# Hybrid gates projected in four column groups of the array and added by a product; diagonal blocks of the lower matrices gathered by ScalarE in place of GpSimd

## The chip, the cores and the metric

The kernel runs on one core of a Trainium2 chip, as one launch. The metric is the device time of the whole launch in microseconds (us), the median of three runs. One further execution was taken by the hardware profiler; all rows of a trace below come from it.

## The reference, cut to what matters here

The program is a six-layer network over 256 tokens of width 1024, in float32. The change lies in its first layer, the hybrid mixer, which works on 256 latent and 256 context tokens together (512 columns, `T2`). There the input is projected by `w_in`; of the projection, 16 columns are the gates of the delta rule, and the keys, values and gates lead to a triangular solve by chunks:

```python
p = a @ w_in                                     # for the latent and the context tokens
ba = p[..., OFF_BA_A:OFF_Q_B].reshape(bsz, n_tok, 2, 2, A_HEADS)
beta = sigmoid(ba[:, :, 0])                      # 8 columns
g = -exp(a_log) * softplus(ba[:, :, 1] + dt_bias)  # 8 columns
...
lower = where(strict, einsum(kb, kc) * decay, 0.0)
sol = triangular_solve(lower + eye, rhs, lower=True, unit_diagonal=True)
```

Everything behind the first layer (feed-forward layers, a conformer convolution, two HGRN mixers, an mLSTM and an S5 mixer) is unchanged.

## The kernel before, in words

Each engine has one instruction queue that it works off in order; semaphores tie the queues together. Weights stream from memory by SyncE (line 4760) in slabs of 1 MB into a ring of six; slab n is issued when the PE has gone past slab n - 6. Products write into seven PSUM banks that are handed out in turn.

In the first layer the input `a` lies as 8 chunks of 128 features by 512 tokens. `HybridProjection` makes 22 column chunks of 128 outputs, numbered n = 0 to 21: 0 to 3 keys, 4 to 7 queries of the attention, 8 and 9 its keys and values, 10 to 13 queries of the delta rule, 14 to 17 its values, 18 to 21 the readout gate. Each is 8 products in float32 (two instructions each in the trace) of 512 or 256 columns. The order of the work is written out by hand in `tensor`, `scalar`, `vector` and `gpsimd`, and other work is hung in after given n:

- after n = 4 on the PE: `gates` (line 1862), 8 products of 72 output columns by 512 tokens, line 1869. Rows 0 to 7 of the result are the decays, rows 64 to 71 the betas. They stand in one table of 128 weight columns in which both 8-column weights lie 64 apart. Then two sums of squares of heads (line 1850);
- on ScalarE, n = 4 ends with the chunk's copy, a SiLU (`silu`, line 1928), a table load (line 1906), a square (line 1936) and the roots of heads 0 and 1 (lines 1944, 1947). n = 5 is the copy of chunk 5 (line 1898), two squares, and `gate_exps` (lines 1955 to 1963), eight activations on the gates. VectorE finishes them in `gate_values` (lines 2009 to 2011). The PE's next step after chunk 6 and its sums is `columns.turn` (line 2235), which waits for that;
- after n = 8, 9, 11 and 13: `lower.products`, the Gram matrices of the keys. VectorE makes the lower matrices of them in `lower.vector`; those of the backward direction are turned by the PE (line 2327) and copied by ScalarE (line 2375). The last turn stands after n = 14;
- `convolve` (lines 2026 and 2028) is a convolution of five taps over each of 12 chunks on VectorE. Convolution 8 reads chunk 14, convolution 9 chunk 15. ScalarE writes their input with the copy of line 1894;
- after n = 11, 13, 15, 17 and within the attention, the PE works off weight slabs of a modulation: products of 32 output columns in four column groups (`part_rows`, line 268 with `silu_cond`);
- `BlockInverse` inverts the diagonal 32x32 blocks of the 32 lower matrices. GpSimd (POOL) clears areas (lines 2451, 2452), waits for the last lower matrix and its turn, gathers the blocks from `l` into `near` by 4 copies of 32 partitions by 1024 elements (line 2476 via `copy`), clears `a` (line 2459), later `b` (line 2463), and scatters the results back (line 2476 again). VectorE transposes what was gathered in `gather` (line 2489), behind convolution 9, and then runs 31 steps (lines 2515, 2516), partly between the rounds of the attention;
- at the end of the projection ScalarE copies chunk 21, does two SiLUs and loads a table (line 1922). The attention begins there with a copy of turned values (line 2154) and the exponentials of the scores (line 2160), each behind VectorE's maximum of them (lines 2208, 2209). VectorE scales the probabilities (lines 2186, 2190), and the PE turns them.

Of the kernel before, what the change touches and what calls it, by code (L numbers as in the profile page):

```python
# [66 lines left out]

VECTORS = [
# [3 lines left out]
    ("hyb_a_log", 1), ("hyb_dt_bias", 1), ("hyb_g_w", KC * 8), ("hyb_beta_w", KC * 8),  # L72
# [12 lines left out]
    ("time", T), ("future", 2 * P),  # L85
# [337 lines left out]
def over_chunks(ap, n):  # L423

    return ap.unsqueeze(1).broadcast_to([ap.shape[0], n, ap.shape[1]])

# [1301 lines left out]
class HybridProjection(Stage):  # L1728
# [7 lines left out]
    def setup(self):  # L1736
# [22 lines left out]
        self.gate_taken, self.gate_exp = k.counter("gate_taken").events(2)  # L1759
# [17 lines left out]
        for n in range(len(self.chunks)):  # L1777
            self.jobs.append(k.job(self.taken[n]))
            if n == 4:
                self.gate_job = k.job(self.gate_taken)  # L1780
            for i in self.sums_after.get(n, ()):
                self.sum_jobs.append(k.job(self.log_ready[i]))
# [9 lines left out]
    def tensor(self, pe):  # L1792
        k = self.k
        front = k.front
        for n, (job, (_, tokens, _)) in enumerate(zip(self.jobs, self.chunks)):
# [23 lines left out]
            if n == 4:  # L1819
                pe.wait_ge(*front.late_vectors)  # L1820
                self.gates(pe)
                pe.wait_ge(k.consts_loaded, 16)
            for i in self.sums_after.get(n, ()):
                self.sum_head(pe, i)
# [37 lines left out]
    def gates(self, pe):  # L1862
# [3 lines left out]
        rows = KC * 8 + 8  # L1866
        w = self.k.v("hyb_g_w", 0, 2 * KC * 8)
        for c in range(KC):
            mm = pe.matmul(job.ap[0:rows, 0:T2], w[:, 8 * c:8 * c + rows], self.a[:, c, :],
                           start=(c == 0), stop=(c == KC - 1))  # L1870
        mm.then_inc(job.full[0], 1)

    def scalar(self, act):
# [4 lines left out]
        for n, (job, (x, tokens, kind)) in enumerate(zip(self.jobs, self.chunks)):  # L1878
# [28 lines left out]
            for i in self.sums_after.get(n + 1, ()):  # L1907
                self.square(act, i)
            if n == 5:
# [10 lines left out]
            if n == 14:  # L1920
                self.lower.take_turned(act, 3)
        act.preload_act_table_set(EXP_LN)
# [26 lines left out]
    def gate_exps(self, act):  # L1949
# [3 lines left out]
        act.wait_ge(*job.full)  # L1953
# [473 lines left out]
class BlockInverse(Stage):  # L2427
# [8 lines left out]
    def setup(self):  # L2436
# [9 lines left out]
        self.gathered, *self.ready = k.counter("blocks_zero").events(3)  # L2446
        self.turned = k.counter("blocks_turned").events(2)

    def gpsimd(self, pool):
        k = self.k  # L2450
        k.pool.link(pool.memset(self.xc, 0.0))
        k.pool.link(pool.memset(k.spare(W_XC, BLOCK * BLOCK)[:, 0:BLOCK * BLOCK:BLOCK + 1], 1.0))
# [20 lines left out]

    def copy(self, pool, q, done, out, x):
# [11 lines left out]
    def gather(self, dve):  # L2486

        dve.wait_ge(*self.gathered)
# [2397 lines left out]
def pack_vectors(i):  # L4886
# [9 lines left out]

    def states(a):
# [8 lines left out]
    v["hyb_beta_w"], v["hyb_g_w"] = small(i["hyb_w_in"][0][:, 2048:2056]), small(i["hyb_w_in"][0][:, 2056:2064])  # L4906
# [93 lines left out]
```

## Time and profile before

| | us |
|---|---|
| median of three runs | 2289.66 (2287.6 to 2290.04) |
| the profiled execution | 2289.95 |
| its span | 2288.1 |
| PE busy | 2221.1 (97%) |
| VectorE busy | 1617.5 (71%) |
| ScalarE busy | 1156.7 (51%) |
| GpSimd busy | 150.9 (7%) |

A row of the timeline gives the start of a group of like instructions in us from the span's start, the time from its first start to its last end, the engine (PE is the matmul side, PEld its weight loads, DVE VectorE, ACT ScalarE, POOL GpSimd, SPq SyncE's queue), the line, the operation, what it writes and reads, its shape and the count. A bracket tells how long the engine sat idle before it and what ended that. Float32 products stand as two instructions each.

### The profile page before, as it was taken

The page shows a single profiled execution, that of the slowest core. Times are in us where ns is not written, and L with a number is a line of the kernel's source. Part 1 is how long each engine was busy: PE and PEld are TensorE (multiplying, and loading weights), DVE is VectorE, ACT ScalarE, POOL GpSimd, SP SyncE. Part 2 cuts the span into 40 slices and gives each one's busy share as a digit, 9 for nine tenths or more (in the row PEclk, how much of TensorE's full clock was granted, in tenths as well). Part 3 has the DMA queues.
Part 4 walks back from the last instruction along what each step waited for, and adds up shares of the span by engine and source line. Part 5 has one row for each costly group of instructions (what it writes and reads, how often), then busy time and mean ns, then how long its engine had stood idle before and what let it go on. Part 6 is the DMA issues. An engine that isn't in the chain of part 4 may idle for free.

```text
span 2288.1 us, 41418 instructions
## 1 busy us (share of the span) xinstructions
PE 2221.1 (97%) x17332; PEld 2045.9 (89%) x17332; DVE 1617.5 (71%) x2749; ACT 1156.7 (51%) x1937; POOL 150.9 (7%) x142
## 2 busy tenths in 40 slices
PE   7999999999999999999999999999999999999998
PEld 3665979998879999999999989997779999999998
DVE  4398667655977655798557787577988557799654
ACT  3425355443365446756345664345556345957343
POOL 0013000000000000000000000015630000000000
PEclk9999999999999999999999999999999999999999
DMA  8248054555244554414554425552024554514552
GB/s 365 74 198 318 25 215 167 186 185 201 93 166 166 185 185 167 182 56 178 182 182 161 147 93 203 184 221 74 19 94 184 184 184 169 183 54 166 185 184 74
DMA packets 50873, 368.46 MB, mean 161 GB/s; under 512 B 5632, under 2 KB 5888, under 8 KB 6528
## 3 DMA queue, kind: packets, MB, share of 16 engines
q1 hardware_dynamic: 50544, 363.72, 43.1%
q8 instruction: 137, 2.24, 0.4%
q10 hardware_dynamic: 144, 2.10, 0.2%
q14 instruction: 48, 0.39, 0.1%
HBM read 364.75 MB, written 1.05 MB: 160 GB/s over the span
## 4 chain that ended last, share of the span: by engine, by line
PE 81%; DVE 11%; ACT 5%; issue 2%; DMA 0%; SPq 0%; DVEq 0%; POOL 0%; ACTq 0%
PE psum L268 67%; DVE weight_rest L262 2%; PE psum L4515 1%; PE psum L3076 1%; PE psum L4516 1%; ACT weight_parts L226 1%; PE psum L4537 1%; PE psum L3710 1%; PE psum L2726 1%; DVE work L2028 1%; PE psum L4551 1%; DVE work L3540 1%; DVE spare L2516 0%; DVE work L2515 0%; DMA weight_ring<-stream_dram 0%
## 5 line engine op out<-in xcount | busy, mean ns | idle before, releaser
L268 PE MATMUL psum<-input_parts,weight_parts 128*128 128x256 f32 x5184 | 931.6, 283 | 6.4 <-DVE work L1495 1.8
L268 PEld LDWEIGHTS psum<-input_parts,weight_parts 128*128 128x128 f32 x5184 | 799.3, 189 | 11.6 <-issue 5.7
L268 PE MATMUL psum<-input_parts,weight_rest 128*128 128x256 f32 x2592 | 732.6, 283 | 0.0
L262 DVE TENSOR_TENSOR weight_rest<-weight_ring,weight_parts 128x1024 fp32r<-128x1024 f32 x528 | 619.9, 1220 | 149.3 <-ACT weight_parts L226 148.9
L226 ACT ACTIVATE weight_parts<-weight_ring 128x1024 fp32r<-128x1024 f32 x540 | 538.0, 1051 | 122.5 <-PE psum L268 121.7
L268 PEld LDWEIGHTS psum<-input_parts,weight_rest 128*128 128x128 f32 x2592 | 487.8, 188 | 0.0
L268 PE MATMUL psum<-hidden_parts,weight_parts 128*128 128x256 f32 x2496 | 450.8, 283 | 2.6 <-DVE weight_rest L262 1.3
L268 PEld LDWEIGHTS psum<-hidden_parts,weight_parts 128*128 128x128 f32 x2496 | 385.0, 189 | 5.9 <-issue 3.4
L268 PE MATMUL psum<-hidden_parts,weight_rest 128*128 128x256 f32 x1248 | 352.1, 282 | 0.0
L268 PEld LDWEIGHTS psum<-hidden_parts,weight_rest 128*128 128x128 f32 x1248 | 234.9, 188 | 0.0
L1479 ACT ACTIVATE work<-psum 128x256 f32<-128x256 f32 x118 | 45.3, 384 | 352.4 <-PE psum L268 350.0
L1499 DVE TENSOR_TENSOR work<-work,psum 128x256 f32<-128x256 f32 x118 | 49.6, 420 | 212.4 <-ACT work L1479 212.2
L268 PE MATMUL psum<-work,weight_ring 128*128 128x256 f32 (+1 forms) x576 | 155.7, 428 | 0.2 <-ACT work L674 0.2
L268 PEld LDWEIGHTS psum<-work,weight_ring 128*128 128x128 f32 x576 | 108.5, 190 | 42.7 <-issue 31.4
L268 PE MATMUL psum<-raw_parts,weight_parts 128*128 128x258 f32 x576 | 109.5, 291 | 2.4 <-DVE raw_parts L697 2.1
L268 PEld LDWEIGHTS psum<-raw_parts,weight_parts 128*128 128x128 f32 x576 | 92.2, 194 | 4.3 <-issue 3.6
L268 PE MATMUL psum<-raw_parts,weight_rest 128*128 128x258 f32 x288 | 82.8, 287 | 0.0
L262 POOL TENSOR_TENSOR weight_rest<-weight_ring,weight_parts 128x1024 fp32r<-128x1024 f32 x12 | 29.0, 2442 | 669.0 <-ACT weight_parts L226 669.0
L268 PE MATMUL psum<-weight_parts,input_parts 128*128 128x256 f32 x384 | 69.2, 283 | 0.0
L268 PE MATMUL psum<-weight_ring,silu_cond 128*32 128x256 f32 x768 | 51.4, 390 | 14.5 <-DMA weight_ring<-stream_dram 12.0
L3141 DVE SCALAR_TENSOR_TENSOR work<-work,vectors 128x256 f32<-128x256 f32 x161 | 64.4, 478 | 0.0
L3774 POOL MEMSET work<- 128x4096 f32 x2 | 7.1, 3530 | 858.5 <-DVE input_parts L945 661.6
(532 smaller groups left out, 2855.9 us busy)
## 6 DMA issues: line engine op xcount, KB each, us to landing
weight_ring<-stream_dram SPq DMA_DIRECT2D x340, 1024.0 KB, 4.8
constants<-constants_dram SPq DMA_DIRECT2D x1, 2304.0 KB, 17.1
work<-s_bc_dram ACTq DMA_DIRECT2D x1, 2048.0 KB, 9.7
work<-ctx_dram SPq DMA_DIRECT2D x1, 1024.0 KB, 5.3
residual<-x_dram SPq DMA_DIRECT2D x1, 1024.0 KB, 7.3
work<-first_dram SPq DMA_DIRECT2D x1, 1024.0 KB, 14.9
out_dram<-residual SPq DMA_DIRECT2D x4, 256.0 KB, 2.1
vectors<-vectors_dram SPq DMA_DIRECT2D x1, 486.5 KB, 14.3
```

The source lines that it names most:

```text
L226: act.activation(self.parts[:, s % SPLITS, cols], self.ring[:, i % RING, cols], ACT.Identity)\
L262: ins = dve.tensor_tensor(self.rest[:, i % RING, cols], self.ring[:, i % RING, cols], self.parts[:, s % SPLITS, cols].bitcast(F32), ALU.su ...
L268: mm = pe.matmul(*args, **kw)
L1479: act.activation(self.hid[:, j % 2, :], job.early.ap[:, 0:T], ACT.Silu).then_inc(self.silu[j][0], 1)
L1499: dve.tensor_tensor(hid, hid, job.ap[:, T:2 * T], ALU.mult).then_inc(self.whole[j][0], 1)
L2028: ins = dve.scalar_tensor_tensor(x, src, w, x, ALU.mult, ALU.add)
L2726: mm = pe.matmul(job.ap[:, h * P:(h + 1) * P], left[:, h, :], right[:, h, :], start=True, stop=True)
L3076: mm = pe.matmul(job.ap[:, 0:T], self.tap(c, at), self.u[:, c, at:at + T], start=(at == first), stop=(at == CONV_C - 1 and c < SHIFTED))
L3141: ins = dve.scalar_tensor_tensor(acc, src, w, acc, ALU.mult, ALU.add)
L3540: ins = dve.tensor_tensor(e[:, :, 0, :], e[:, :, 0, :], halves(k_all, b)[:, :, 0, :], ALU.mult)
L3710: mm = pe.matmul(job.ap[:, at:at + width], (e if b > 1 else kk)[:, h, cols], later[:, first:first + width // b, :], start=True, stop=True)
L4515: pe.matmul(out, k.c("ident"), t1[:, part, :], start=True, stop=False)
```

## The change

The gates' 8 products now have 32 weight columns each (16 that are used and 16 of the next chunk's or the next vector's) and go to column groups 0 to 3 by chunk modulo 4, so that each group holds a partial sum of two chunks. ScalarE copies the four partial sums into `gate_strips` at the end of n = 4, between the square and the roots. After chunk 5 the PE adds them by one product with a constant 128x72 matrix into the same bank, whose rows then are as before. `gate_exps` waits for that sum. The gather of the diagonal blocks goes from GpSimd to ScalarE (`collect`, 4 activations), after the last turned lower matrix is taken at n = 14; GpSimd clears `a` at once after its waits. The constants grow by 72 columns, and the scratch area for dynamic DMAs shrinks from 1024 to 64.

```diff
@@ VECTORS, CONSTANTS
-    ("hyb_a_log", 1), ("hyb_dt_bias", 1), ("hyb_g_w", KC * 8), ("hyb_beta_w", KC * 8),
+    ("hyb_a_log", 1), ("hyb_dt_bias", 1), ("hyb_gates_w", KC * 16),
-    ("time", T), ("future", 2 * P),
+    ("time", T), ("future", 2 * P), ("gate_sum", GATE_ROWS),
@@ new function
+def gate_strips(k, pe, out, name, x, ready=None):
+    for c in range(KC):
+        at = STRIP * (c % 4)
+        if ready:
+            pe.wait_ge(*ready[c])
+        mm = pe.matmul(out[at:at + STRIP, :], k.v(name, 16 * c, STRIP), x[:, c, :], start=(c < 4), stop=(c >= 4),
+                       tile_position=(0, at))
+    return mm
@@ HybridProjection.tensor
+            if n == 5:
+                self.sum_gates(pe)
@@ HybridProjection.gates
-        rows = KC * 8 + 8
-        w = self.k.v("hyb_g_w", 0, 2 * KC * 8)
-        for c in range(KC):
-            mm = pe.matmul(job.ap[0:rows, 0:T2], w[:, 8 * c:8 * c + rows], self.a[:, c, :],
-                           start=(c == 0), stop=(c == KC - 1))
-        mm.then_inc(job.full[0], 1)
+        gate_strips(self.k, pe, job.ap[:, 0:T2], "hyb_gates_w", self.a).then_inc(job.full[0], 1)
+
+    def sum_gates(self, pe):
+        pe.wait_ge(*self.gate_copied)
+        pe.matmul(self.gate_job.ap[0:GATE_ROWS, 0:T2], self.k.c("gate_sum"), self.gate_strips, start=True, stop=True)\
+          .then_inc(self.gate_summed[0], 1)
@@ HybridProjection.scalar
+            if n == 4:
+                act.wait_ge(*self.gate_job.full)
+                act.activation(self.gate_strips, self.gate_job.ap[:, 0:T2], ACT.Identity)\
+                   .then_inc(self.gate_copied[0], 1)
             if n == 5:
                 self.gate_exps(act)
@@
             if n == 14:
                 self.lower.take_turned(act, 3)
+                self.blocks.collect(act)
@@ gate_exps
-        act.wait_ge(*job.full)
+        act.wait_ge(*self.gate_summed)
@@ BlockInverse.gpsimd
-        l = k.spare(W_L, MATS, P)
-        for q in range(BLOCKS):
-            at = self.quarter(q)
-            self.copy(pool, q, self.gathered, self.near[at, :, :], l[at, :, at])
         k.pool.link(pool.memset(self.a, 0.0))
@@
+    def collect(self, act):
+        k = self.k
+        act.wait_ge(*self.lower.l_ready[-1])
+        act.wait_ge(*self.lower.turned[-1])
+        l = k.spare(W_L, MATS, P)
+        for q in range(BLOCKS):
+            at = self.quarter(q)
+            ins = act.activation(self.near[at, :, :], l[at, :, at], ACT.Identity)
+        ins.then_inc(self.gathered[0], 1)
@@ gather
+        dve.wait_ge(*self.unit_ready)
         dve.wait_ge(*self.gathered)
@@ kernel
-    nc = _bacc.Bacc("TRN2", target_bir_lowering=False, num_devices=1, dynamic_dma_scratch_size=1024)
+    nc = _bacc.Bacc("TRN2", target_bir_lowering=False, num_devices=1, dynamic_dma_scratch_size=64)
```

## Rows read from the trace of the kernel before

**Rows 1.** The page, part 4: the chain that ended last, by engine.
```profile
PE 81%; DVE 11%; ACT 5%; issue 2%; DMA 0%; SPq 0%; DVEq 0%; POOL 0%; ACTq 0%
```
**Rows 2.** Timeline of the PE, 60 to 81 us: the gates, and the turn behind them.
```profile
60.51 7.03 PE L1869 MATMUL psum<-work,vectors 128*72 128x512 f32 x16
67.38 1.88 PE L1850 MATMUL psum<-work,constants 128*128 128x512 f32 x4
...
80.05 0.63 PE L2235 MATMUL psum<-constants,work 8*128 8x8 f32 x8 [1.74 <-DVE work L2011]
```
**Rows 3.** Timeline of the PE, 117 to 120 us, and the weight loads of line 268 there (ns min/median/max).
```profile
117.75 1.93 PE L268 MATMUL psum<-weight_ring,silu_cond 128*32 128x256 f32 x32
119.62 3.72 PE L268 MATMUL psum<-work,weight_ring 128*128 128x256 f32 x16
```
```profile
L268 PEld LDWEIGHTS psum<-weight_ring,silu_cond x26: 109/110/110, 117.8 to 119.1; 128*32 128x32 f32 x26
```
**Rows 4.** Timeline of ScalarE, 68 to 75 us.
```profile
68.44 0.69 ACT L1944 ACTIVATE work<-psum,epsilons 128x512 f32<-128x512 f32 x1 [4.31 <-PE psum L1850]
...
72.75 0.38 ACT L1898 ACTIVATE work<-psum 128x256 f32<-128x256 f32 x1 [1.73 <-PE psum L268]
...
73.86 0.66 ACT L1955 ACTIVATE work<-psum,vectors 8x512 f32<-8x512 f32 x1
```
**Rows 5.** Timeline of VectorE, 141 to 156 us, and line 2028 within convolution 9 alone.
```profile
141.86 0.49 DVE L2026 TENSOR_SCALAR work<-work,vectors 128x512 f32<-128x512 f32 x1 [0.30 <-ACT work L1894]
142.38 5.22 DVE L2028 SCALAR_TENSOR_TENSOR work<-work,vectors 128x512 f32<-128x512 f32 x4
149.87 2.48 DVE L2026 TENSOR_SCALAR work<-work,vectors 128x512 f32<-128x512 f32 x1 [2.28 <-ACT work L1894]
```
```profile
L2028 DVE SCALAR_TENSOR_TENSOR work<-work,vectors x4: 751/752/752, 152.4 to 154.7; 128x512 f32<-128x512 f32 x4
```
**Rows 6.** Timeline of GpSimd, 140 to 330 us.
```profile
143.14 5.36 POOL L2476 COPY spare<-spare 32x1024 f32<-32x1024 f32 x4 [97.41 <-ACT spare L2375]
148.56 3.51 POOL L2459 MEMSET work<- 128x4096 f32 x1
```
**Rows 7.** Timeline of ScalarE, 149 us.
```profile
149.24 0.60 ACT L1894 ACTIVATE work<-psum 128x512 f32<-128x512 f32 x1 [6.27 <-PE psum L268]
```
**Rows 8.** The page, part 5 (a ScalarE copy of 1024 elements), and line 2476: GpSimd's scatter (ns min/median/max).
```profile
L226 ACT ACTIVATE weight_parts<-weight_ring 128x1024 fp32r<-128x1024 f32 x540 | 538.0, 1051 | 122.5 <-PE psum L268 121.7
```
```profile
L2476 POOL COPY work<-spare x8: 1933/1971/2222, 207.3 to 221.8; 32x1024 f32<-32x1024 f32 x8
```
**Rows 9.** Timeline of ScalarE, 180 to 185 us.
```profile
180.91 0.38 ACT L1898 ACTIVATE work<-psum 128x256 f32<-128x256 f32 x1 [2.03 <-PE psum L268]
...
182.35 1.28 ACT L1922 ACT_TABLE_LOAD   x1
183.64 0.60 ACT L2154 ACTIVATE work<-psum 128x512 f32<-128x512 f32 x1
184.45 0.66 ACT L2160 ACTIVATE psum<-psum,columns 128x512 f32<-128x512 f32 x1 [0.21 <-DVE columns L2209]
```
**Rows 10.** The chain that ended last, from 185 us, in order of time.
```profile
185.26 0.17 DVE columns L2186
```
**Rows 11.** Timeline of the PE, 181 to 210 us.
```profile
181.24 1.13 PE L2119 MATMUL psum<-work 64*128 64x512 f32 x4
...
209.89 1.13 PE L2119 MATMUL psum<-work 64*128 64x512 f32 x4 [1.14 <-DVE work L2199]
```
**Rows 12.** Who SyncE's queue waited for, 130 to 232 us (us in total, times, longest).
```profile
SPq L4760 <- PE psum L268: 96.2, 26, 14.2
```
**Rows 13.** The page, part 5: products of the three-term form by their moving tile.
```profile
L268 PE MATMUL psum<-input_parts,weight_parts 128*128 128x256 f32 x5184 | 931.6, 283 | 6.4 <-DVE work L1495 1.8
...
L268 PE MATMUL psum<-hidden_parts,weight_parts 128*128 128x256 f32 x2496 | 450.8, 283 | 2.6 <-DVE weight_rest L262 1.3
...
L268 PE MATMUL psum<-raw_parts,weight_parts 128*128 128x258 f32 x576 | 109.5, 291 | 2.4 <-DVE raw_parts L697 2.1
```

More of the change, by code:

```diff
@@ L65 @@
 ROUND = 12582912.0
+GATE_ROWS = 72
 VECTORS = [
@@ L1758, in setup @@
         self.conv_ready = k.counter("conv_ready").events(12)
-        self.gate_taken, self.gate_exp = k.counter("gate_taken").events(2)
+        self.gate_copied, self.gate_taken, self.gate_exp = k.counter("gate_taken").events(3)
+        self.gate_strips = k.area(H_GATE + 2 * T2, T2)
         self.gates_ready = self.columns.gates_ready
@@ L1779, in setup @@
             if n == 4:
+                self.gate_summed = k.bank_full[k.jobs % BANKS]
                 self.gate_job = k.job(self.gate_taken)
+                self.gate_summed = self.gate_summed.event()
             for i in self.sums_after.get(n, ()):
@@ L2445, in setup @@
         self.near = k.spare(W_PROD, BLOCK, BLOCK)
-        self.gathered, *self.ready = k.counter("blocks_zero").events(3)
+        self.gathered = k.counter("lower_turned").event()
+        self.unit_ready, *self.ready = k.counter("blocks_zero").events(3)
         self.turned = k.counter("blocks_turned").events(2)
@@ L2451, in gpsimd @@
         k.pool.link(pool.memset(self.xc, 0.0))
-        k.pool.link(pool.memset(k.spare(W_XC, BLOCK * BLOCK)[:, 0:BLOCK * BLOCK:BLOCK + 1], 1.0))
+        pool.memset(k.spare(W_XC, BLOCK * BLOCK)[:, 0:BLOCK * BLOCK:BLOCK + 1], 1.0).then_inc(self.unit_ready[0], 1)
         pool.wait_ge(*self.lower.l_ready[-1])
         pool.wait_ge(*self.lower.turned[-1])
-        l = k.spare(W_L, MATS, P)
-        for q in range(BLOCKS):
-            at = self.quarter(q)
-            self.copy(pool, q, self.gathered, self.near[at, :, :], l[at, :, at])
         k.pool.link(pool.memset(self.a, 0.0))
@@ L4895, in small, with both @@
         return np.asarray(w).reshape(KC, P, 8).transpose(1, 0, 2).reshape(P, KC * 8)
+    def both(a, b):
+        return np.stack([a.reshape(P, KC, 8), b.reshape(P, KC, 8)], 2).reshape(P, KC * 16)
     def states(a):
@@ L4905, in pack_vectors @@
     v["hyb_a_log"], v["hyb_dt_bias"] = rows(i["hyb_a_log"]), rows(i["hyb_dt_bias"])
-    v["hyb_beta_w"], v["hyb_g_w"] = small(i["hyb_w_in"][0][:, 2048:2056]), small(i["hyb_w_in"][0][:, 2056:2064])
+    v["hyb_gates_w"] = both(small(i["hyb_w_in"][0][:, 2056:2064]), small(i["hyb_w_in"][0][:, 2048:2056]))
     v["hgrn_norm_w"] = chunks(i["hgrn_norm_w_2"])
@@ L4966, in pack_constants @@
     c["future"] = np.concatenate([np.where(t[:, None] <= t[None, :], 0.0, FUTURE), np.zeros((P, P))], 1)
+    c["gate_sum"] = np.zeros((P, GATE_ROWS))
+    for r in range(8):
+        c["gate_sum"][r::STRIP, r] = c["gate_sum"][8 + r::STRIP, 64 + r] = 1.0
     for name, size in CONSTANTS:
```

## The prediction

> **What bounds the kernel now.** I read the page's chain first: 81% of the chain that ended last is the PE's, 11% VectorE's [rows 1]. Over the whole run the products set the time, so what the change can give is a head start: the first layer hands over earlier by some microseconds, and what follows moves with it. For the size I went through the first layer in order of time, chain beside the timelines of all engines, and asked at each hand-over who came last.
>
> Four stretches matter. From 60 to 115 us the PE leads. The gates hold it from 60.51 to 67.38, 6.87 us, and its one pause is 1.74 us at 80.05, where the turn waits for VectorE's last gate value [rows 2]. From 115 to 142 us VectorE leads, fed by the PE and ScalarE without any input from outside that stretch. From 142 the last turn and chunk 15 are the PE's again, then convolution 9 and the block steps are VectorE's; chunks 16 to 21 run on the PE meanwhile without a pause. The two meet at 183 to 185 us, at the first round of the attention [rows 9 to 11]. From there VectorE leads to 209.89, where the PE takes over [rows 11]. Weights don't bind here: between 130 and 232 us, SyncE waited 96.2 of 102 us for the PE to free a slab, in a ring six deep [rows 12].
>
> **The change part by part.** *The gates' products.* Removed: 16 instructions of 512 columns, 6.87 us. Added: 16 of 512 columns in four groups. The nearest rows are the modulation's products, the same form (128 rows, 32 columns, four groups in turn, float32): 32 instructions of 256 columns, so the same number of streamed columns, hold the PE from 117.75 to 119.62, which is 1.87 us [rows 3]. Saved: 6.87 - 1.87 = 5.00 us. From above the cost is bounded by no overlap at all, 6.87; from below by nothing less than the row, since four groups are all there are.
>
> A rule speaks against this. In the row, 32 products with weight loads of 0.110 us each finish in 1.87 us [rows 3]; one after another the loads alone would be 3.5 us, so loads into one column group run beside products in another. The Trainium skill (page "TensorE: Matmul & The Clock Gate", section "Part 3: Packing small matmuls — row/col tiling") says that weight loads overlap with products in flight only when the row group differs, and here all four groups use all rows. By that rule the loads would add to the products; this case's trace disagrees with it. I keep it as a rival, priced below from rows.
>
> *The copy of the strips.* One ScalarE activation of 128x512 from PSUM, 0.60 us by the like row at 149.24 [rows 7]. It stands behind the square, which ended at 68.44 - 4.31 = 64.1 [rows 4]; the strips are there at 60.51 + 1.87 = 62.4, so it waits for nothing. ScalarE sat idle 4.31 us behind that square, and covers it. The roots behind it need the PE's head sums (now at 63.3) and are four activations of at most 0.69 [rows 4], so ScalarE is free at 67.4 or before. Chunk 5's copy, at 72.75 before [rows 4], is due at 67.75: cover 0.35 us. Without that cover the excess goes onto the gates' path one for one.
>
> *The sum.* Two instructions of 512 columns at 0.43 us (6.87/16), 0.86 us on the PE, behind chunk 5. It waits for the copy, done at 64.7, while chunk 5 ends at 67.7: no wait. `gate_exps` began 1.1 us after chunk 5's copy began, because of two squares (73.86 against 72.75 [rows 4]), and the sum is ready 0.9 us after chunk 5: nothing, or 0.1. The PE reaches the turn 5.00 - 0.86 = 4.1 us earlier and the gate values come 5.0 earlier, so the pause of 1.74 us shrinks to 0.9, and the turn starts at 75.05. Costed at nothing; the cover is that pause. The head start behind the turn is 5.0 us.
>
> *Moved on to 142 us.* Nothing there hangs on a clock of its own, so VectorE's stretch too moves by 5.0.
>
> *The gather on ScalarE.* Removed from GpSimd: 4 copies, 5.36 us [rows 6]. Added to ScalarE: 4 activations of 1024 elements per partition. The nearest row is 1.05 us for 1024 [rows 8]; the other end is GpSimd's slowest scatter of the same shape, 2.22 [rows 8]. I take 1.05, since it is the same engine: 4.2 us. Behind it in ScalarE's queue is the copy of chunk 15, before which the engine sat idle 6.27 us [rows 7]; 4 x 2.22 = 8.9 would exceed that by 2.6. VectorE's transpose needs the blocks only behind convolution 9, some 10 us after the turned matrix. Cost nothing on my value.
>
> *GpSimd's clearing comes earlier.* Before, it ran from 148.56 for 3.51 us [rows 6], to 152.07. Convolution 9 opened at 149.87, and its first tap took 2.48 us instead of the 0.49 of convolution 8's: it ended just behind the clearing [rows 5]. That is 2.0 us of stall on the path. Now the clearing starts at 143.1 in old time and ends at 146.6, during convolution 8. If it blocked the remaining taps wholly, these would end at about 146.7 + 3 x 0.75 = 149.0, and VectorE would still wait for chunk 15 until 149.87 [rows 5]. So nothing either way, and the 2.0 us go. VectorE is 5.0 + 2.0 = 7.0 us ahead from convolution 9 on. That convolution 8 gets faster (its four taps took 5.22 us beside the copies, against 4 x 0.75 [rows 5]) is worth nothing: it fills VectorE's wait of 2.28 us.
>
> The Trainium skill (page "SBUF — State Buffer", section "SBUF: two separate sides") calls this a lock held for a whole instruction, and has a tap with two SBUF inputs contend only with a GpSimd operation that reads SBUF. By that the clearing would not hold up convolution 8 at all; this trace has no such pair.
>
> *What is late next.* Most of those 2.0 us meet the attention's first round. ScalarE comes to the first exponential by chunk 21's copy (180.91, waiting for the PE), two SiLUs, the table load and the copy of turned values at 183.64 [rows 9]. That queue is only 5.0 ahead. It ended at 184.24, and the exponential started at 184.45, having waited 0.21 us for VectorE's maximum [rows 9]. With VectorE 7.0 ahead (or held by the scores at 181.24 [rows 11], 6.5 ahead), the exponential starts when ScalarE is free: 5.0 + 0.2 to 0.3 (queued activations overlap by 0.1) earlier. VectorE's next step is the reciprocal at 185.26 [rows 10], behind it. So the head start is 5.25 us, and 1.7 of the 2.0 are idle time. Then VectorE leads, and at 209.89 the PE gets it as it is [rows 11].
>
> *The rest.* The larger constants are 37 KB more in a transfer that was done long before its first use; nothing. Behind the first layer all waits are relative.
>
> *Sum.* 2289.95 for the profiled execution (span 2288.1) less 5.25 is 2284.7. That execution lay 0.29 above the median of 2289.66, so the forecast is 2284.4.
>
> **The rivals.**
> - *VectorE's gain is kept.* If ScalarE's tail doesn't bind as I read it, VectorE goes on from the scores, 6.5 ahead: 2283.2. For it: the margin rests on 0.21 us of one trace. Against: PE, ScalarE and table load are one unbroken queue.
> - *Weight loads in series.* 16 x 0.110 = 1.76 us are added to the 1.87 [rows 3]; saved are 3.24, and with the 0.25 the time is 2286.2. That is the page's rule above as a mechanism of this kernel. Against: rows 3 themselves.
> - *The strips don't run side by side: the change does not do what it says.* The PE keeps 6.87 us, the added sum vanishes in the pause of 1.74 us, and only the 0.25 at the exponential is left: 2289.4. Against: rows 3 again; for it: the moving side is `a` and not the ring.
> - *The gain is partly taken back.* ScalarE's gather at 2.22 us a copy delays chunk 15 by 2.6 us; the stall of 2.0 that went and the idle 1.7 of VectorE nearly cover that too, but a second such place, in a queue that I held relative, would cost 2 to 3 us: 2287.
> - *Slower: addresses.* 72 constants more (288 bytes a partition) and a smaller scratch area move every buffer allocated behind. The products from `raw_parts`, which has rows of 258 elements, take 291 ns against 283 for 256 [rows 13]; two columns at 283/256 are 2.2 ns of that, the other 5.8 could be where the rows start. The three-term products from `input_parts` and `hidden_parts`, (5184 + 2496) x 3/2 = 11,520 with the third term [rows 13], would lose 11.5 us for each ns. From 0.46 ns the head start is gone, from 0.86 the kernel is 0.2% slower; at 1 ns it is 2295.9. Against: products from tiles at quite different places (`input_parts`, `hidden_parts`) have the same mean of 283 [rows 13].
>
> **How the numbers follow.** About 0.2%, 4.6 us, is what a measurement of this kernel can tell from no change: the line is 2285.1. The forecast has 0.64, gain kept 0.10, loads in series 0.06, no overlap 0.06, taken back 0.09, addresses 0.05. The forecast lies 0.7 us inside the line, and medians of this kernel scatter by about 1, so three quarters of its 0.64 count as faster (0.48). With 0.10 and a rest of 0.01 that is 0.59 faster; slower are the addresses, 0.05; same is 0.36. The range takes in the forecast with its scatter, the gain kept, loads in series and half of what is taken back: 2282.6 to 2287.2.
>
> **What the profile of the changed kernel would show.** The gates as 16 products of 32 columns in 1.87 us from 60.5; the sum at about 67.7 for 0.86; the turn at 75.05 behind 0.9 of idle PE; four ScalarE activations of 1.05 us from 138 to 142.3; the clearing on GpSimd from 138.1; convolution 9's first tap at 144.9 with 0.49; the exponential at 179.2, with no idle time of ScalarE before it and VectorE waiting; the second score round of the PE's last stretch (209.89) at 204.6. The prediction is wrong if the gates take over 2.5 us, if the turn starts after 75.5, if chunk 15's copy comes late, or if products behind 310 us have a mean other than 283 ns.

## The result, and the profile after

| | before | after |
|---|---|---|
| median, us | 2289.66 (2287.6 to 2291.8, 5 runs) | 2267.88 (2266.86 to 2271.12, 5 runs) |
| the profiled execution, us | 2289.95 | 2266.86 |
| its span, us | 2288.1 | 2265.1 |
| PE busy, us | 2221.1 | 2196.9 |

The ratio is 0.9909 (0.9895 to 0.9924): 21.8 us are gone, where 5.25 were forecast. The rows below show that the forecast's own 5 us came within 0.2 us, and that the other 17 lie elsewhere.

The first layer. Timeline of the PE of the kernel after, from 60 us: start, us from the first start to the last end, engine, line, operation, tiles, shape, count, and in brackets the idle time before it.

```profile
60.92 1.92 PE L437 MATMUL psum<-work,vectors 128*32 128x512 f32 x16
62.78 1.98 PE L1869 MATMUL psum<-work,constants 128*128 128x512 f32 x4
64.60 3.62 PE L271 MATMUL psum<-work,weight_ring 128*128 128x256 f32 x16
68.05 1.02 PE L1890 MATMUL psum<-work,constants 128*72 128x512 f32 x2
68.91 1.02 PE L1869 MATMUL psum<-work,constants 128*128 128x512 f32 x2
...
75.55 0.63 PE L2260 MATMUL psum<-constants,work 8*128 8x8 f32 x8 [0.88 <-DVE work L2036]
```

The gates hold the PE from 60.92 to 62.78, 1.86 us, where they held it 6.87 [rows 2]; the sum takes 68.91 - 68.05 = 0.86; the pause ahead of the turn went from 1.74 [rows 2] to 0.88. Then timelines of VectorE, ScalarE and GpSimd from 137 to 181 us:

```profile
137.88 3.11 DVE L2053 SCALAR_TENSOR_TENSOR work<-work,vectors 128x512 f32<-128x512 f32 x4
145.39 0.49 DVE L2051 TENSOR_SCALAR work<-work,vectors 128x512 f32<-128x512 f32 x1 [4.39 <-ACT work L1914]
```
```profile
138.58 4.25 ACT L2504 ACTIVATE spare<-spare 32x1024 f32<-32x1024 f32 x4
144.76 0.60 ACT L1914 ACTIVATE work<-psum 128x512 f32<-128x512 f32 x1 [1.93 <-PE psum L271]
...
179.16 0.60 ACT L2179 ACTIVATE work<-psum 128x512 f32<-128x512 f32 x1
179.65 0.66 ACT L2185 ACTIVATE psum<-psum,columns 128x512 f32<-128x512 f32 x1
```
```profile
138.61 3.51 POOL L2481 MEMSET work<- 128x4096 f32 x1 [92.64 <-ACT spare L2400]
```

ScalarE's four copies take 4.25 us and end 1.93 us before chunk 15 is there, so they hold nothing up. The clearing now lies under convolution 8, and convolution 9's first tap takes 0.49 us instead of 2.48 [rows 5]. VectorE waits 4.39 us for chunk 15 instead of 2.28. The first exponential starts right behind ScalarE's copy, with no idle time before it [rows 9]. How far the head start had grown when the first layer's work of this kind was over is read at the score products behind the attention, first of before, then of after:

```profile
230.93 2.92 PE L2621 MATMUL psum<-work 128*128 128x128 f32 x24 [1.16 <-issue]
```
```profile
226.12 2.13 PE L2655 MATMUL psum<-work 128*128 128x128 f32 x17 [1.16 <-issue]
```

That is 4.81 us earlier. The kernel after began its conditioning products 0.32 us later (before, then after). Its first weights had come 0.30 us sooner (first product at 11.74 us, against 12.04), but the trace's first record of the full clock is later, at 16.37 us against 15.33, and two products at 15.3 us took 1.22 us against 0.70:

```profile
42.19 1.10 PE L1644 MATMUL psum<-work,silu_cond 128*32 128x64 f32 x64
```
```profile
42.51 1.10 PE L1658 MATMUL psum<-work,silu_cond 128*32 128x64 f32 x64
```

So the change's own gain in the first layer is 4.81 + 0.32 = 5.13 us. Over the whole run the products still set the time, as in before [rows 1]; the chain of after, by engine:

```profile
PE 79%; DVE 12%; ACT 6%; issue 2%; DMA 0%; SPq 0%; DVEq 0%; POOL 0%; ACTq 0%
```

The rest of the gain comes behind it, and in two forms. First, the long stretches of products run faster. The page of after, part 5 (busy us, mean ns of one, idle before):

```profile
L271 PE MATMUL psum<-input_parts,weight_parts 128*128 128x256 f32 x5184 | 919.0, 281 | 6.8 <-DVE work L1509 1.8
...
L271 PE MATMUL psum<-hidden_parts,weight_parts 128*128 128x256 f32 x2496 | 446.4, 282 | 2.6 <-DVE weight_rest L265 1.3
...
L271 PE MATMUL psum<-raw_parts,weight_parts 128*128 128x258 f32 x576 | 106.0, 285 | 3.6 <-DVE raw_parts L711 3.2
```

The first two groups had 931.6 and 450.8 us of busy time, 283 ns each, and the third 109.5 and 291 [rows 13]. The code of these products is the same. I call them three-term products: each float32 operand is split into two rounded parts, and three products of parts make one; each of the three is counted. Products overlap, so their pace is better read where the PE never stops: two windows of 50 us, (x) being instructions, of before and then of after (columns: the window, its length in us, then the busy us of the PE, its weight loads, VectorE, ScalarE and GpSimd, then the granted clock, DMA share, GB/s).

```profile
1110.00:1160.00 50.00, 50.00 (x419) 50.00 (x418) 28.86 (x45) 19.79 (x27) 0.00 (x0) 1.00 0.49 178
2150.00:2200.00 50.00, 50.00 (x419) 50.00 (x418) 30.27 (x45) 20.52 (x27) 0.00 (x0) 1.00 0.51 183
```
```profile
1110.00:1160.00 50.00, 50.00 (x429) 50.00 (x428) 31.98 (x44) 21.97 (x28) 0.00 (x0) 1.00 0.53 190
2150.00:2200.00 50.00, 50.00 (x429) 50.00 (x428) 31.57 (x45) 22.16 (x28) 0.00 (x0) 1.00 0.53 184
```

419 products became 429 in the same time, at the same full clock. Over the whole trace, the mean from the start of one three-term product to the start of the next (pauses and stretches at the lower clock, 135 ns or more, left out) is 119.27 ns before and 117.93 after. Over 12,960 such products that is 17.4 us of PE time. The lead of after over before, read at the starts of the same instructions in both traces, grew: 4.8 us at 300 us of the trace, 6.6 at 350, 10.0 at 700, 12.6 at 950, 16.0 at 1250, 18.9 at 1550, 19.4 at 2060, 22.9 at 2250. Between 1550 and 2060 us it hardly grew, although 2,748 of the products lie there; what held it there was not examined.

Second, the lead also grew in two steps, 1.5 us at 343 and 1.6 at 677 us. There the granted clock fell to its lower level in before, for 3.4 and 6.8 us, and not in after. Windows at 341 to 347 us, before and after (of before two more ahead of them):

```profile
335.00:338.00 3.00, 2.24 (x18) 1.84 (x16) 3.00 (x4) 2.99 (x3) 0.00 (x0) 1.00 0.08 33
338.00:341.00 3.00, 2.41 (x10) 1.74 (x10) 2.96 (x7) 1.56 (x5) 0.00 (x0) 1.00 0.00 0
341.00:344.00 3.00, 1.42 (x8) 1.17 (x7) 2.85 (x9) 2.07 (x6) 0.00 (x0) 0.83 0.03 5
344.00:347.00 3.00, 3.00 (x18) 3.00 (x18) 3.00 (x9) 2.08 (x6) 0.00 (x0) 0.60 0.92 292
```
```profile
341.00:344.00 3.00, 3.00 (x27) 3.00 (x27) 3.00 (x9) 2.38 (x8) 0.00 (x0) 1.00 0.42 175
344.00:347.00 3.00, 3.00 (x27) 3.00 (x27) 2.86 (x7) 2.35 (x4) 0.00 (x0) 1.00 0.00 0
```

A PE that was busy for all of 3 us made 18 products at a mean clock of 0.60, and 27 at 1.00.

### The profile page after: what moved, and what is told of

It is laid out like the page before. It is cut to its first block, busy times and chain, and to the rows that moved or that the text cites. A ratio compares the mean times of both kernels' runs of the same rounds, so it can differ in the third digit from the quotient of the medians.

```text
span 2265.1 us, 41425 instructions
## 1 busy us (share of the span) xinstructions
PE 2196.9 (97%) x17334; PEld 2023.4 (89%) x17334; DVE 1613.2 (71%) x2749; ACT 1161.0 (51%) x1942; POOL 146.1 (6%) x138
## 3 DMA queue, kind: packets, MB, share of 16 engines
q8 instruction: 137, 2.24, 0.4%
HBM read 364.78 MB, written 1.05 MB: 162 GB/s over the span
## 4 chain that ended last, share of the span: by engine, by line
PE 79%; DVE 12%; ACT 6%; issue 2%; DMA 0%; SPq 0%; DVEq 0%; POOL 0%; ACTq 0%
PE psum L271 66%; DVE weight_rest L265 2%; PE psum L4549 1%; PE psum L3110 1%; ACT weight_parts L229 1%; PE psum L4550 1%; PE psum L4571 1%; PE psum L3744 1%; PE psum L2760 1%; PE psum L4585 1%; DVE work L3574 0%; DMA weight_ring<-stream_dram 0%; PE psum L4168 0%; DVE work L1385 0%; DVE work L1381 0%
## 5 line engine op out<-in xcount | busy, mean ns | idle before, releaser
L271 PE MATMUL psum<-input_parts,weight_parts 128*128 128x256 f32 x5184 | 919.0, 281 | 6.8 <-DVE work L1509 1.8
L229 ACT ACTIVATE weight_parts<-weight_ring 128x1024 fp32r<-128x1024 f32 x540 | 538.1, 1051 | 119.3 <-PE psum L271 118.5
L271 PE MATMUL psum<-work,weight_ring 128*128 128x256 f32 (+1 forms) x576 | 155.7, 428 | 0.2 <-ACT work L688 0.2
```

What stands on the lines that cost most here:

```text
L229: act.activation(self.parts[:, s % SPLITS, cols], self.ring[:, i % RING, cols], ACT.Identity)\
L271: mm = pe.matmul(*args, **kw)
```

## The experiments

My theory after the result: the faster products come from where the buffers lie. The smaller scratch area moves everything down by 960 bytes a partition, and the 72 constants move what is behind them up by 288. The rival: the changed first layer is itself the cause, through the clock or through a different phase of engines and transfers. For this, the start of the rounded weights (`weight_parts`) and of the moving operands (`input_parts`), in bytes of a partition, and the distance from the weights' start to the moving operands' start, modulo 128. "Spacing" is the mean from start to start as above:

| kernel | weights | moving | distance modulo 128 | products in 1110 to 1160 us | mean spacing, ns |
|---|---|---|---|---|---|
| before | 50304 | 117760 | 0 | 419 | 119.27 |
| old_addresses | 50304 | 117760 | 0 | 419 | 119.28 |
| gather_alone | 50304 | 117760 | 0 | 419 | 119.44 |
| gates_alone_again | 50304 | 117760 | 0 | 419 | 119.37 |
| distance_0_moved | 49376 | 117088 | 0 | 419 | 119.37 |
| after | 49344 | 117088 | 32 | 429 | 117.93 |
| new_addresses | 49344 | 117088 | 32 | 428 | 118.05 |
| distance_32 | 49376 | 117760 | 32 | 427 | 117.64 |
| changed_distance_32 | 49376 | 117760 | 32 | 427 | 117.62 |
| only_weights_moved | 49344 | 117760 | 64 | 427 | 117.69 |
| distance_64_moved | 50304 | 117184 | 64 | 427 | 117.64 |
| changed_distance_64 | 49344 | 117760 | 64 | 426 | 117.20 |
| only_parts_moved | 50304 | 117088 | 96 | 424 | 118.37 |

`weight_rest` lies 49,152 bytes ahead of `weight_parts`, so it has the same remainder; `hidden_parts` lies 28,672 bytes behind `input_parts`, also a multiple of 128. Every shift was made with unused buffers, the place of two small tables (`mods`) and the scratch size, and no instruction was changed by one. The window counts one stretch, which holds other products in a faster kernel, so it tells slow from fast but doesn't rank the fast ones as the mean spacing does. `gates_alone` has the old addresses too; its trace is missing here for the reason given with it.

**The change at the old addresses.**

```diff
 after:
+        sb("pad_before_weights", [P, 48])
+        self.mods = [sb(f"modulation{i}", [P, COND, 2]) for i in range(2)]   # before the ring
...
+        sb("pad_before_work", [P, 120])
         self.work_n = 25600
```

> The changed kernel whole, with buffers moved so that the weight buffers, the input, hidden and raw parts and the whole work area start at the same addresses as in the kernel before (only the residual and small tables differ). Theory 1, addresses: the products' mean spacing depends on where their buffers start, and that made the 17 us that the prediction lacked. Then the three-term products go back to 283 and 291 ns in the page and only the head start of the first layer is left, about 5.1 us: 2284.5. Theory 2, the gain comes from the edits themselves (order of the first layer, another alignment of engines in time further on): it stays at 2268.

Measured: 2280.59 us (2278.78 to 2283.85) beside 2288.36 (2285.19 to 2291.79) of before, ratio 0.9965 (0.9952 to 0.9979). The whole change is in it, and it gains 7.8 us instead of 21.8. That is 2.7 more than the 5.1 I expected; the section on the prediction comes back to it. The three-term products are back at before's 119.28 ns, in this window of old_addresses:

```profile
1110.00:1160.00 50.00, 50.00 (x419) 50.00 (x418) 30.29 (x45) 21.70 (x29) 0.00 (x0) 1.00 0.52 184
```

`raw_parts` lies where it lay in before, but its products have 286 ns here and not before's 291 [rows 13]. The 291 was thus for the most part not a matter of place: a third of those products stand around 343 and 677 us, where before's clock fell. Without the 30 of the 576 that took over 400 ns the mean of before is 283.4.

**Before at the new addresses.**

```diff
 before:
+    ("unused", 72),
+    c["unused"] = np.zeros((P, 72))
-    nc = _bacc.Bacc("TRN2", target_bir_lowering=False, num_devices=1, dynamic_dma_scratch_size=1024)
+    nc = _bacc.Bacc("TRN2", target_bir_lowering=False, num_devices=1, dynamic_dma_scratch_size=64)
```

> The kernel before with 72 unused columns of constants and the scratch area at 64, so that every buffer starts where the changed kernel has it, and none of the edits to gates and gather. Theory 1, addresses: products at 281 and 285 ns, about 17 us faster, 2272.8, while the first layer up to 300 us keeps its length. Theory 2, edits: 2289.7.

Measured: 2274.18 (2272.12 to 2276.47), ratio 0.9934 (0.9921 to 0.9946): 14.2 us less without one instruction of the change.

```profile
1110.00:1160.00 50.00, 50.00 (x428) 50.00 (x428) 30.04 (x45) 19.84 (x27) 0.00 (x0) 1.00 0.51 189
```

By the medians the two effects add up: 7.8 us (the change at old addresses) and 14.2 (the addresses alone) make 22.0, and the whole is 21.8. The rival, that the new first layer speeds up what follows, falls for these 14 us.

**Which of the buffers, and how.** Before, with the scratch area of 64 and pads that bring only the moving operands, or only the weights, to their new place.

```diff
 only_parts_moved:
+        sb("pad_before_weights", [P, 48])
+        self.mods = [...]                        # before the ring
+        sb("pad_before_work", [P, 24])
 only_weights_moved:
+        sb("pad_before_work", [P, 240])
```

> The kernel before with the weight buffers where they were and the work area (input, hidden and raw parts) 672 bytes lower, as in the changed kernel: it starts at a multiple of 64 bytes plus 32, the weights at a multiple of 64. If the start of the moving parts decides, or their distance to the weights modulo 64, it is as fast as new_addresses, 2273. If the start of the weights decides, it stays at 2289.7.

> The kernel before with the work area where it was and the weight buffers 960 bytes lower, as in the changed kernel; both start at multiples of 64 bytes. If the start of the weights decides, 2273. If the start of the moving parts decides, or the distance modulo 64, it stays at 2289.7.

Measured: 2279.65 (2277.35 to 2280.34), ratio 0.9956 (0.9943 to 0.997), with only the moving operands elsewhere; 2272.97 (2272.46 to 2275.54), ratio 0.9931 (0.9918 to 0.9945), with only the weights. Either helps by itself, so it is no property of one buffer's place. I had taken the distance modulo 64 for what counts, and both refuted that. only_weights_moved has 0 modulo 64, as before, and should have stayed at 2289.7; only_parts_moved has 96, which is 32 modulo 64 as in after, and came 6.7 us above my 2273. Modulo 128 the values so far were in order: 0 slow, 96 half way, 32 and 64 fast.

**The distance against the place.** Two kernels tell them apart: both have the weights at the same new place, and the moving operands once at the old and once at the new one.

```diff
 distance_32:
+        sb("pad_before_weights", [P, 8])
+        sb("pad_before_work", [P, 232])
 distance_0_moved:
+        sb("pad_before_weights", [P, 8])
+        sb("pad_before_work", [P, 64])
```

> The kernel before with the work area at its old address and the weight buffers at 224, so that the moving parts lie 32 bytes past the weights modulo 128, as in the changed kernel, but both at other absolute places. Theory, distance: the mean spacing of the three-term products is that of the changed kernel, 117.8 ns against 119.2, products of 281 ns in the page, 2274. Theory, absolute place of the weights modulo 128: unlike both seen so far, 96; no value is foretold by it.

> The kernel before with the work area at the address that the changed kernel gives it (117088) and the weight buffers at 224: both moved, distance 0 modulo 128 as in the kernel before. Theory, distance: slow as before, 283 ns, 2288. Theory, absolute place of either: fast, since the work area lies as in the changed kernel and the weights are off the 128 multiple, 2274.

Measured: distance_32 2267.61 (2265.43 to 2270.5), ratio 0.9913 (0.9898 to 0.9927). distance_0_moved 2288.94 (2287.42 to 2292.24, 10 runs), ratio 1.0005 (0.9995 to 1.0014). In the second, weights and moving operands both lie elsewhere than in before, and nothing is gained; the moving operands lie even where after has them. Windows of distance_32, then of distance_0_moved:

```profile
1110.00:1160.00 50.00, 50.00 (x427) 50.00 (x426) 29.83 (x45) 20.79 (x28) 0.00 (x0) 1.00 0.52 182
```
```profile
1110.00:1160.00 50.00, 50.00 (x419) 50.00 (x418) 28.86 (x45) 19.82 (x27) 0.00 (x0) 1.00 0.49 176
```

So for these products the distance of the two operands decides between slow and fast, and not the place of either. distance_32 was 6 us faster than the 2274 that I expected: its spacing is 117.64 against new_addresses' 118.05 at the same distance, which is 5.3 us over 12,960 products. What makes that difference within one distance I can't say.

**The two parts of the change one by one**, both at before's addresses. First the gather alone (before with `collect` on ScalarE and its semaphores, and nothing else).

> The kernel before with the gather on ScalarE alone; all buffers at their old addresses. The clearing on GpSimd comes earlier, the first tap of convolution 9 goes from 2.48 to 0.49 us. My theory: ScalarE's queue ahead of the first exponential keeps all but 0.2 to 0.3 us of the 2.0, so that the PE's first product after 225 us (230.93 before) is 0.3 us earlier. Rival: the whole 2.0 or 1.6 us arrive there. In the median neither is to be told from the 2288 of before unless a reduced stretch of the granted clock comes or goes.

Measured: 2289.49 (2286.58 to 2290.95, 10 runs) beside 2288.28 (25 runs), ratio 1.0001 (0.9992 to 1.0011): no gain that can be measured. Its trace bears out why, first VectorE at convolution 9, then ScalarE at the exponential:

```profile
149.50 0.49 DVE L2027 TENSOR_SCALAR work<-work,vectors 128x512 f32<-128x512 f32 x1 [4.38 <-ACT work L1894]
```
```profile
183.27 0.60 ACT L2155 ACTIVATE work<-psum 128x512 f32<-128x512 f32 x1
183.77 0.66 ACT L2161 ACTIVATE psum<-psum,columns 128x512 f32<-128x512 f32 x1
```

The stall of 2.0 us is gone, and the exponential starts 0.68 us earlier than in before (184.45 [rows 9]), of which 0.36 had been there at the gates (60.15 against 60.51 [rows 2]). The gather's own gain is 0.3. The other 1.7 of the 2.0 us became idle time of VectorE, as the forecast had it: from 152.7 to 185.0 us it was busy 30.19 us in before, without a pause, and 28.47 here, with two pauses:

```profile
182.10 0.69 DVE L2209 TENSOR_REDUCE columns<-psum 128x1 f32<-128x512 f32 x1 [0.99 <-PE psum L2120]
184.57 0.16 DVE L2187 RECIPROCAL columns<-columns 128x1 f32<-128x1 f32 x1 [0.80 <-ACT psum L2161]
```

The rival that VectorE keeps its gain falls.

Then the gates alone (after with the gather back on GpSimd, at the old addresses), two times: the first time's profiled execution took 4757.35 us, with a mean of 453 ns for the products that take 283 in before, for a reason that the record doesn't show, and its trace is not used.

> The changed kernel with the gather back on GpSimd, and weight buffers and work area at the addresses of the kernel before. The first layer is 5.0 us shorter (less 0.3 at most), so about 2283.5 and PE products of the three-term form at 283 ns. Rival: the medians of old_addresses were lower than 5.1 us by the clock (its executions show 0.998, those of before 0.995 or 0.996), then this one too comes out at 2281.

> gates_alone once more, for its trace: gates in column groups, gather on GpSimd, old addresses. The first layer's end (first product after 225 us, 230.93 before, against the start of the gates) is 4.8 us earlier relative to the gates' start, all of it from the gates; the first tap of convolution 9 keeps its stall of 2 us.

Measured: 2282.55 (ratio 0.9979, 0.9969 to 0.9989; the nine executions other than that one 2281.13 to 2286.98), and 2281.08 (2280.68 to 2286.38; ratio 0.9974, 0.996 to 0.9989), which is 5.7 and 7.4 us less than before. At 300 us of its trace gates_alone_again leads before by 5.20 us, of which 0.38 were there at the start: 4.82 for the gates in the first layer, as expected; the first tap of convolution 9 keeps its 2.48 us. So the first layer's 5.13 us are the gates' 4.8 and the gather's 0.3. The lead is 6.8 at 350, since the clock stays up there:

```profile
341.00:344.00 3.00, 3.00 (x27) 3.00 (x26) 3.00 (x8) 2.38 (x7) 0.00 (x0) 1.00 0.36 153
344.00:347.00 3.00, 3.00 (x27) 3.00 (x26) 2.86 (x8) 2.15 (x3) 0.00 (x0) 1.00 0.00 0
```

**The change with the better distances.**

```diff
 changed_distance_32 (after):
+        sb("pad_before_weights", [P, 8])
+        sb("pad_before_work", [P, 160])
 changed_distance_64 (after):
+        sb("pad_before_work", [P, 168])
 distance_64_moved (before, scratch area of 64):
+        sb("pad_before_weights", [P, 48])
+        self.mods = [...]                        # before the ring
+        sb("pad_before_work", [P, 48])
```

> The changed kernel with weight buffers at 224 and the work area at 117760, as in distance_32 (moving parts 32 bytes past the weights modulo 128, at other absolute places than the changed kernel). Distance theory with the head start of the first layer: distance_32's 2267.6 less 5.1 is 2262.5. If that run owed part of its time to the clock and not to the spacing, it is 2266 to 2268, as the changed kernel.

> The changed kernel with the work area at 117760 and the weights where it has them, 192: distance 64 modulo 128. only_weights_moved had this distance and 2273.0; less 5.1 is 2267.9. The products with weight_parts as the moving side were at 277 ns there against 283; they are few (576), so it may be some 1 to 2 us below the changed kernel, not more.

> The kernel before with the weight buffers at their old address (1152) and the work area at 117184, a multiple of 64 bytes as before: distance 64 modulo 128, made by moving the other side than only_weights_moved did. Distance theory: products at 280 ns, about 427 products in 50 us of a steady stretch, 2273. Theory that the weights' start decides: 283 ns, 419, 2288.

Measured: changed_distance_32 2265.44 (2263.56 to 2267.21), ratio 0.9895 (0.988 to 0.991). changed_distance_64 2263.79 (2256.21 to 2268.45), ratio 0.9886 (0.9868 to 0.9903), the fastest kernel here by its median: 4.1 us under after by one pad of 672 bytes, though its own runs spread over 12 us and the intervals of the two overlap. Neither came where I expected it. changed_distance_32 lies 2.9 us above 2262.5, only 2.2 below distance_32 instead of 5.1, at the same spacing; its traced execution has one fall of the clock more (four against three). changed_distance_64 lies 4.1 us below my 2267.9, with the smallest spacing of all, 117.20. That is the scatter within which these medians can be read. distance_64_moved 2272.61 (2271.59 to 2274.13), ratio 0.993 (0.9916 to 0.9943), which confirms distance 64 at another pair of places: only_weights_moved has the same distance and 2272.97.

Distance 64 is told apart from 32 by one group of the page, the 384 products in which the rounded weights are the moving side. Here it is of before, of changed_distance_64 and of distance_64_moved:

```profile
L268 PE MATMUL psum<-weight_parts,input_parts 128*128 128x256 f32 x384 | 69.2, 283 | 0.0
```
```profile
L271 PE MATMUL psum<-weight_parts,input_parts 128*128 128x256 f32 x384 | 66.1, 276 | 0.9 <-DVE weight_rest L265 0.9
```
```profile
L268 PE MATMUL psum<-weight_parts,input_parts 128*128 128x256 f32 x384 | 66.1, 276 | 0.6 <-DVE weight_rest L262 0.6
```

These, with their counterparts on `weight_rest`, have a spacing of 113.4 ns at distance 64 in all three kernels, and 116.9 at 96, 118.3 or 120.0 at 32 and 119.3 to 120.0 at 0. Here the sides are swapped: counted from the stationary to the moving operand, the table's 32 is 96 and its 96 is 32. Counted so, these products have the same order as the others: 64 and 32 fastest, then 96, then 0.

## Why the prediction was wrong, point by point

*The gates:* 5.00 us were forecast and 6.87 - 1.86 = 5.01 measured. The modulation's products were the right row to go by. The Trainium skill's rule that weight loads overlap with products only across row groups (page "TensorE: Matmul & The Clock Gate", section "Part 3: Packing small matmuls — row/col tiling") is contradicted by this row too: its 16 loads took up to 0.110 us each, in series 1.76 us, and loads and products took 1.86 together. The rival "loads in series" falls, and with the 1.86 us also "no overlap".

*Copy, sum and pause:* 0.86 us for the sum and a pause of 0.9 were forecast, 0.86 and 0.88 came. The turn is 80.05 - 75.55 + 0.32 = 4.8 us earlier against 5.0; some 0.1 us went ahead of the strips (60.51 to 60.92, less the late start of 0.32), and 0.1 in the sums of squares behind them (1.98 us against 1.88 [rows 2]).

*The gather, the clearing and what is late next:* 4 x 1.05 forecast, 4.25 came; the stall went and ScalarE's queue became what is late; 0.25 us forecast as its worth, 0.3 in gather_alone. That convolution 8 might be held up by the clearing was allowed for and did not happen (3.11 us for four taps). By the Trainium skill (page "SBUF — State Buffer", section "Who interferes with whom") an operation with two SBUF inputs contends with GpSimd only where that reads SBUF, and both cases here agree: 3.11 us beside the clearing, 5.22 beside GpSimd's copies [rows 5].

*The sum of the first layer,* 5.25 us, is 5.13 in the trace. Its two parts came where they were forecast, 4.8 us from the gates and 0.3 from the gather, so this part was right by its mechanism and not by luck.

*What failed is the step "The rest".* It priced the larger constants by their transfer alone and gave nothing for the moved buffers. One of the prediction's own signs of being wrong, a mean other than 283 ns behind 310 us, showed it at once: 281 and 282. The trace of before didn't show that price, and so it should have been bounded from both sides. The rival "addresses" had the mechanism's place and its lever, 11.5 us for each ns of the three-term products, but was written as a loss only, without a reason that excludes a gain, and with a chance of 0.05. What the runs showed in place of that nothing is 1.34 ns on 12,960 products, 17.4 us of PE time, and 14.2 us of the kernel's time with the addresses alone (new_addresses). The rival counted 11,520 products; those from `raw_parts` and those with the weights as moving side make up the rest. The listed chances add up to 1.00 without the "rest of 0.01".

Both rows that I weighed for it misled me. That `input_parts` and `hidden_parts` have the same mean [rows 13] was taken as evidence against; they lie a multiple of 128 bytes apart, so they can't show any effect of the distance. And the 5.8 ns of `raw_parts` that spoke for it were mostly clock: old_addresses has 286 ns with the tile in the same place.

*A second, smaller term was left out: the clock.* "Behind the first layer all waits are relative" says nothing of the stretches at the lower clock level, which are not waits. The change at old addresses gained 7.8 us by the medians, 5.1 of them in the first layer; its trace leads before by 5.1 at 300 us (start of the trace taken off) and steps up by 1.5 at 343, by 1.6 at 677 and by 1.6 at 2043 us, where before's clock fell and its own did not. Of the eight kernels without the four column groups, each one's profiled execution shows such a stretch at 82 or 343 us; of the five with them and a usable trace, four show none there and changed_distance_32 one at 338. At 82 us the PE has just come out of the turn's pause, which the change cut from 1.74 to 0.88. That the shorter pause is the cause is only argued, from one execution of each kernel. Over the whole trace there is no such order: ahead of the last 10 us the clock fell once in distance_0_moved and twice in gather_alone, both without column groups, and four times in changed_distance_32.

The granted clocks of all executions, each listed to 0.001, bear on how much of this belongs to the change. Their mean is 0.9964 in after (5) and 0.9966 in gates_alone (9), and 0.9963, 0.9967 and 0.9967 in before, in its three series beside the experiments. So these two show no gain in clock, and gates_alone gained 5.7. Higher were old_addresses, 0.9974 against 0.9963, and gates_alone_again, 0.9975 against 0.9967, and these two gained 7.8 and 7.4. Since the lower level is half of the full one, 0.001 of the mean over 2,288 us is 2.3 us (an estimate from these rows): old_addresses owes some 2.5 of its 7.8 us to the clock, and 5.3 are left. new_addresses ran at 0.9956 against 0.9963, some 1.6 us the other way, so at equal clock its 14.2 would be 15.8, which is also 12,960 times its 119.27 - 118.05 ns. So the clock fits the differences between executions; that the change keeps it up is not shown.

The account: first layer 5.1, addresses 14.2 by their own median and about 15.8 at equal clock. That leaves 2.5 or 0.9 of the 21.8 us for the clock and the scatter of the medians, which the runs don't part.

*What stays open.* Why the distance counts was not shown. A product streams its moving rows from SBUF while the next weights are loaded from it (PEld is busy for 50.00 of 50 us in each window above), and the two reads meeting in some unit would fit; no run takes the one away and keeps the other. A clash with the writes of ScalarE and VectorE, which fill the weight buffers meanwhile, isn't excluded either. Distances modulo more than 128 weren't tried, nor steps finer than 32 bytes by a shift. But rows of `raw_parts` are 1,032 bytes long, so its chunks lie 8 bytes apart modulo 128 and meet many distances in every kernel. Their spacing is 120.1 to 120.3 ns with the buffers at distance 0 and 119.5 to 120.0 otherwise, while that of `input_parts` and `hidden_parts` together goes from 119.2 to 119.4 down to 117.2 to 118.3. By its two columns more a product from `raw_parts` should take 119.2 x 258/256 = 120.1 ns at distance 0 (an estimate), so in before the chunks at other distances gained nothing that shows. For rows of this length the rule by the distance is not confirmed. Nor is it explained why kernels of one distance differ by 0.4 ns.

## What to carry to other kernels

An edit of a table, a scratch size or an allocation moves every buffer behind it, and in a kernel that the PE bounds this can outweigh the edit's purpose: run the old kernel with the new addresses and the new kernel with the old ones, and the two parts separate in two runs. When the trace doesn't show what a side effect costs, bound it in both directions, and ask of a row that seems to speak against it whether it could have shown the effect at all. And before a gain is put down to the clock, compare the granted clocks of all executions, not only of the traced ones. Where products set the time, try a few distances between the stationary and the moving operands: 32 or 64 bytes modulo 128 instead of 0 was worth 14 to 21 us of 2289 here, without a changed instruction.

## What the runs showed of the hardware that was not expected

- Three-term products of 128x128 by 256 columns (864 of the 12,960 have 258) start on average every 119.3 to 119.4 ns where moving and stationary operand lie at a distance of 0 modulo 128 bytes in their partitions, every 117.6 to 118.1 ns at 32, 117.2 to 117.7 at 64 and 118.4 at 96 (13 traces). The Trainium skill (page "SBUF — State Buffer", section "Who interferes with whom") gives the PE two independent read ports and says that it never waits on anyone. The 13 traces don't test it against other engines; they show a pace that depends on the place of the PE's own two operands. The float32 products from `work` and `weight_ring`, two instructions each, show nothing of it: their group on the page is the same in both kernels, 155.7 us for 576. The line of after:

```profile
L271 PE MATMUL psum<-work,weight_ring 128*128 128x256 f32 (+1 forms) x576 | 155.7, 428 | 0.2 <-ACT work L688 0.2
```
- In each of the 13 traces the granted clock falls from 2.4 to 1.2 GHz in one to four places ahead of the last 10 us, mostly for 3.4 us. Ahead of before's fall at 343 us the PE had been busy 2.24, 2.41 and 1.42 us of 3 each. Before's falls at 343, 677 (6.8 us long) and 2043 us cost it 1.5, 1.6 and 1.6 us against old_addresses. In 3 us of which most lay at the lower level (mean clock 0.60) 18 products were made instead of 27.
- Sixteen products with weights of 128 rows by 32 columns, each 512 columns long, in four column groups in turn, take 1.86 us where 16 of 72 columns in one place took 6.87: a factor of 3.7 for four groups.
